# The product of the bias table with the one-hot rows moves from ahead of the first attention scores to among the first idle products

## The chip, the cores and the metric

The kernel runs on one core of a Trainium2 chip. The core has five engines, each with its own queue of instructions: TensorE (PE, matrix products), VectorE (DVE), ScalarE (ACT), GpSimd (POOL) and SyncE (SP, which here only issues transfers). Engines wait for one another by semaphores. Sixteen DMA engines move data between HBM and SBUF. The metric is the device time of one execution in microseconds (us).

## The reference, cut to what matters

Two transformer blocks of width 1024 over 256 tokens. The first has a short convolution and a compressed, selected and windowed attention; the second a differential attention, a gated linear attention and a pooling mixer; each ends in a gated feed-forward part. The changed part computes one small thing of the second block, the bias of a score by the distance of query and key:

```python
bias_by_dist = rel_bias[t5_bucket(jnp.arange(S))]          # 256 distances x 4 heads
...
dist = jnp.arange(q0, kend)[:, None] - jnp.arange(kend)[None, :]
bias = bias_by_dist[jnp.clip(dist, 0, S - 1)].astype(jnp.float32)
s = s + jnp.transpose(bias, (2, 0, 1))[None, :, None]
s = jnp.where(dist[None, None, None] >= 0, s, -1e30)
```

## The kernel before, in words

All order is written out by hand, one instruction list per engine, in `program`. TensorE holds x transposed (AA) and multiplies it by weights that come from HBM in units of up to 1 MB. SyncE issues the units in the order of the list `units` into a ring of four buffers (RAW, `NRAW`). A unit is issued when the unit four places ahead has been split (`split_lo`). ScalarE makes a unit's rounded high part (HI, `hi`, L538) and VectorE the rest (LO, `lo`, L1002), each in two halves, into rings of three; TensorE waits for the half it needs (`unit_ready`).

The first units are, in order: keys of the windowed branch (0), the two for the compressed blocks (1, 2), the gates (3, 192 KB), query weights (4), the first layer of the key compression (5, 6), query weights (7), the value compression (8, 9), query weights (10, 11) and values (12). TensorE goes through them in the function under `@block.tensor`: `queries(0, ...)` uses unit 4, `hidden(0)` units 5 and 6, `queries(1, ...)` unit 7, `hidden(1)` units 8 and 9, `queries(2, ...)` unit 10. After `values(U_VALS, ...)` the attention of the first block begins, in which projections (units 13 and on) fill the time between its small steps.

Until x is there, TensorE has nothing to do and runs idle products (`idle(n)`, L1639): 14, then the two that spread the gain `g_mix` over the partitions (L1646), then 13, then the first turns of the normalized x (L1633).

The bias table takes this way. GpSimd loads the constant one-hot rows (OH, 33 x 384) and the table (REL, 32 x 4; its row 32 is set to -1e30 for distances below zero). TensorE multiplies them (L1781) into 4 x 384 bias values in bank B[0], behind the values and ahead of the first scores. ScalarE writes them back into the first four rows of OH (L649). GpSimd then issues `bias_rows` (L456), a transfer that writes each of the four rows 128 times to HBM:

```python
e.wait_ge(setup, HMASK)
e.wait_ge(rel_sb, 1)
e.dma_start(bias_rows.rearrange("h r n -> h (r n)").rearrange("h (r n) -> h r n", n=ROW),
            OH[0:4, :].unsqueeze(1).to_broadcast([4, 128, ROW])).then_inc(bias_moved, 16)
```

It is read back skewed (L468) when the scores of the first attention are done, at 225.9 us. On GpSimd's queue all instructions run in order: first `ones`, `ident` and ROOT, then loads of small rows (VR), the first root (`root(1, ...)`, the inverse root of x's mean square), more loads, masks, the loads of OH and REL, later small loads, two loads of gains (GB, 512 KB each as written), the memsets of `hmask`, and `bias_rows`.

Of the kernel before, what the change touches and what calls it, by code (L numbers as in the profile page):

```python
# [17 lines left out]
NEG = -1.0e30  # L18
# [3 lines left out]
ROW = 384  # L22
# [37 lines left out]
def program(nc, A, out):  # L60
    with ExitStack() as ctx:
# [3 lines left out]
        def sem(name):  # L65
            return ctx.enter_context(nc.semaphore("s_" + name))
# [86 lines left out]
        rows_in, first_in, second_in = sem("rows_in"), sem("first_in"), sem("second_in")  # L153
        FIRST_IN, SECOND_IN = 80, 64
        bias_moved, out_done = sem("bias_moved"), sem("out_done")

        setup = sem("setup")
        ONE, IDENT, HALF, IDENTB, MASKF, MASKC, KC0, VB0, UP0, GMASK, FAR, HMASK = 1, 3, 4, 6, 8, 10, 11, 12, 13, 16, 17, 22
        gate_sb = sem("gate_sb")
# [19 lines left out]
        ck_pe, ck_sb, cv_pe, cv_sb = sem("ck_pe"), sem("ck_sb"), sem("cv_pe"), sem("cv_sb")  # L179
        rel_pe, rel_sb = sem("rel_pe"), sem("rel_sb")  # L180

        score_pe, masked_sb, most_sb, exp_sb = sem("score_pe"), sem("masked_sb"), sem("most_sb"), sem("exp_sb")
# [199 lines left out]
        def _(e):  # L382
# [10 lines left out]
            def root(n, dst, src, k=2):  # L393

                e.wait_ge(mean_sb, n)
                e.tensor_tensor(dst, src, ROOT[:, 0:k], ALU.pow).then_inc(root_sb, 1)

            e.dma_start(VR[0:12, :], A["conv_w"][0].rearrange("k (c p) -> (k c) p", p=128)).then_inc(rows_in, 16)
            e.dma_start(VR[12:28, :], A["cmp_pos_k"][0].rearrange("(l a) d -> l (a d)", a=2)).then_inc(rows_in, 16)
            e.dma_start(VR[28:44, :], A["cmp_pos_v"][0].rearrange("(l a) d -> l (a d)", a=2)).then_inc(rows_in, 16)  # L400
            e.dma_start(VR[44:46, :], A["pool_scale_2"][0, :].rearrange("(c p) -> c p", p=128)).then_inc(rows_in, 16)
            e.dma_start(VR[46:47, :], A["gla_gate_b_2"]).then_inc(rows_in, 16)
            e.wait_ge(setup, HALF)
            root(1, ST[:, 6:8], ST[:, 4:6])
# [28 lines left out]
            for h in range(2):  # L433
                e.affine_select(out=gmask[h * 64:h * 64 + 64, :], in_=gmask[h * 64:h * 64 + 64, :], compare_op=ALU.is_ge,
                                fill=0.0, base=0, pattern=[[1, 64]], channel_multiplier=-1).then_inc(setup, 1)
            e.dma_start(OH[:, :], A["c_onehot"]).then_inc(first_in, 16)
            e.dma_start(REL[0:32, :], A["rel_bias_2"]).then_inc(first_in, 16)
            e.wait_ge(setup, GMASK)
            e.memset(REL[32:33, :], NEG).then_inc(setup, 1)
            e.dma_start(LV[:, :, :], A["lambda_vecs_2"][0].rearrange("a d -> (a d)").partition_broadcast(128)  # L440
# [7 lines left out]
            gain(1, A["g_ffn"][0, :])  # L448
            e.wait_ge(setup, FAR)
            e.memset(hmask[:, :], 0.0).then_inc(setup, 1)  # L450
            e.wait_ge(setup, FAR + 1)
            for h in range(4):
# [71 lines left out]
        def _(e):  # L524
# [40 lines left out]
            def keys(br, c):  # L565
                e.wait_ge(keys_pe, 2 * br + c + 1)
                e.activation(KT[:, br, c, :], B[c][:, 0:S], ACT.Copy).then_inc(keys_sb, 1)

            def values(br, t):
                e.wait_ge(vals_pe, 2 * br + t + 1)  # L570
                e.activation(VV[:, br, t, :], B[t][:, 0:256], ACT.Copy).then_inc(vals_sb, 1)

            keys(0, 0)
            hi(2, 0)
# [72 lines left out]
            values(0, 1)  # L647
            e.wait_ge(rel_pe, 1)
            e.activation(OH[0:4, :], B[0][0:4, 0:ROW], ACT.Copy).then_inc(rel_sb, 1)  # L649

# [905 lines left out]
        def _(e):  # L1556
# [79 lines left out]
            def idle(n):  # L1636

                for _ in range(n):
                    e.matmul(B[7][:, 0:128], ones[:, :], ones[:, :], start=True, stop=True)  # L1639
# [7 lines left out]
            x.then_inc(gain_pe, 1)  # L1647
            idle(13)
            e.wait_ge(setup, IDENT)
# [127 lines left out]
            for t in range(2):  # L1777
                values(U_VALS, 0, t)
            e.wait_ge(setup, FAR)
            take(0, rel_sb, 1)  # L1780
            e.matmul(B[0][0:4, 0:ROW], REL[:, :], OH[:, :], start=True, stop=True).then_inc(rel_pe, 1)  # L1781

# [478 lines left out]
```

## Time and profile before

| | |
|---|---|
| device time, median of 3 runs | 747.46 us (746.82 to 747.47) |
| span of the profiled execution | 745.2 us (the page gives no other time of it) |
| TensorE busy | 740.4 us, 99% |
| VectorE busy | 518.0 us, 70% |
| ScalarE busy | 416.4 us, 56% |
| GpSimd busy | 66.5 us, 9% |
| chain that ended last | TensorE 97%, VectorE 2%, ScalarE 1% |
| moved by DMA | 131.26 MB, mean 176 GB/s; 266, 297, 311 and 274 GB/s in the first four of 40 slices |

The span runs from the first to the last instruction of the profiled execution. A row of a timeline gives the start in us from the span's start, the length, the engine, the line and what it writes and reads; "xN" are records merged into one row. An fp32 product leaves two records. The idle time ahead of a row stands in brackets, with what ended it. A DMA's "us to landing" runs from its issue until its semaphore is complete.

### The profile page before, as it was taken

To read this page: it belongs to the slowest core of one execution; us is meant where nothing else is said; L and a number is where in the kernel's file an instruction comes from. 1 tells how busy PE (TensorE), PEld (TensorE's weight loads), DVE (VectorE), ACT (ScalarE), POOL (GpSimd) and SP (SyncE) were. 2 spreads that over 40 slices of the span, in tenths; PEclk is the share of its full clock that TensorE was granted. 3 is DMA by queue.
4 is the path that set the end of the run, shared out by engine and by line. 5 is a ranking of instruction groups with operands and counts; after the bars stand their busy time and mean duration, and the time that the engine had idled before them with its cause. 6 is when DMAs were issued, how large, how long until landed. Compare 5 with 4: busy or idle time off the path is not lost.

```text
span 745.2 us, 11582 instructions
## 1 busy us (share of the span) xinstructions
PE 740.4 (99%) x4563; PEld 641.4 (86%) x4563; DVE 518.0 (70%) x834; ACT 416.4 (56%) x788; POOL 66.5 (9%) x103
## 2 busy tenths in 40 slices
PE   9999999999999999999999999999999999999998
PEld 8999999877888888888888888887888888888886
DVE  5784677885756678887367757898667777447762
ACT  5575557556463455565356546597646656345640
POOL 6300000000010000430000004400100000000000
PEclk9999999999999999999999999999999999999999
DMA  8998444343455546766656461735355655656611
GB/s 266 297 311 274 85 109 153 114 128 123 146 170 197 167 152 222 198 213 228 188 172 212 171 226 54 251 124 174 111 168 170 191 204 174 222 170 188 207 57 56
DMA packets 99209, 131.26 MB, mean 176 GB/s; under 512 B 5357, under 2 KB 79163, under 8 KB 99156
## 3 DMA queue, kind: packets, MB, share of 16 engines
q1 hardware_dynamic: 96564, 125.58, 52.6%
q0 software_dynamic: 2304, 4.43, 2.7%
q8 instruction: 36, 0.59, 0.3%
q10 hardware_dynamic: 288, 0.52, 0.2%
q14 instruction: 17, 0.14, 0.1%
HBM read 128.68 MB, written 1.84 MB: 175 GB/s over the span
## 4 chain that ended last, share of the span: by engine, by line
PE 97%; DVE 2%; ACT 1%; issue 0%; POOL 0%; POOLq 0%
PE B L1626 39%; PE B L1592 22%; PE B L1597 11%; PE B L1581 11%; PE B L1805 2%; PE B L1852 2%; PE B L1815 2%; PE B L1639 1%; PE B L1685 1%; PE B L1633 1%; DVE LO L1002 1%; PE B L1808 1%; PE B L1832 1%; PE B L1730 1%; PE B L1791 0%; PE B L1729 0%
## 5 line engine op out<-in xcount | busy, mean ns | idle before, releaser
L1002 DVE TENSOR_TENSOR LO<-RAW,HI 128x1024 fp32r<-128x1024 f32 x236 | 282.5, 1236 | 101.0 <-ACT HI L538 100.5
L1626 PE MATMUL B<-HI,AA 128*128 128x512 f32 (+1 forms) x960 | 286.8, 376 | 0.3 <-DVE AA L1008 0.2
L538 ACT ACTIVATE HI<-RAW 128x1024 fp32r<-128x1024 f32 (+1 forms) x240 | 237.2, 1038 | 63.1 <-PE B L1626 58.2
L1626 PEld LDWEIGHTS B<-HI,AA 128*128 128x128 f32 x960 | 175.7, 188 | 33.8 <-issue 1.6
L1592 PE MATMUL B<-AA,HI 128*128 128x512 f32 x704 | 179.2, 393 | 0.0
L1626 PE MATMUL B<-LO,AA 128*128 128x512 f32 (+1 forms) x480 | 178.6, 372 | 0.0
L1592 PEld LDWEIGHTS B<-AA,HI 128*128 128x128 f32 x704 | 126.8, 189 | 23.0 <-issue 0.7
L1626 PEld LDWEIGHTS B<-LO,AA 128*128 128x128 f32 x480 | 90.6, 189 | 14.6
L1597 PEld LDWEIGHTS B<-AA,LO 128*128 128x128 f32 x704 | 96.6, 190 | 7.1
L1597 PE MATMUL B<-AA,LO 128*128 128x256 f32 x704 | 98.8, 282 | 0.0
L1581 PE MATMUL B<-AA,HI 128*128 128x256 f32 x448 | 83.3, 287 | 0.0
L1581 PEld LDWEIGHTS B<-AA,HI 128*128 128x128 f32 x448 | 69.8, 191 | 1.1 <-issue 0.4
L1581 PE MATMUL B<-AA,LO 128*128 128x256 f32 x224 | 63.4, 283 | 0.0
L1581 PEld LDWEIGHTS B<-AA,LO 128*128 128x128 f32 x224 | 42.9, 191 | 0.0
L663 ACT ACTIVATE PR<-B,SM 128x128 f32<-128x128 f32 (+1 forms) x64 | 26.3, 427 | 27.6 <-DVE SM L1135 27.6
L793 ACT ACTIVATE SGC<-SGC 128x256 f32<-128x256 f32 x44 | 16.8, 418 | 28.3 <-DVE SGC L1329 28.2
L804 ACT ACTIVATE AA<-SGC 128x256 fp32r<-128x256 f32 x44 | 16.7, 418 | 27.9 <-DVE SGC L1339 27.9
L787 ACT ACTIVATE SGC<-B 128x256 f32<-128x256 f32 x44 | 15.7, 372 | 22.5 <-PE B L1592 22.5
L798 ACT ACTIVATE SGC<-B 128x256 f32<-128x256 f32 x44 | 15.5, 371 | 19.7 <-PE B L1592 19.7
L1135 DVE TENSOR_REDUCE SM<-B 128x2 f32<-128x512 f32 (+1 forms) x24 | 15.4, 683 | 15.2 <-PE B L1808 15.2
L674 ACT ACTIVATE PT<-B 128x512 f32<-128x512 f32 x24 | 14.4, 599 | 18.4 <-PE B L1815 8.8
L1324 DVE TENSOR_TENSOR SGC<-B,SGC 128x256 f32<-128x256 f32 x44 | 17.6, 418 | 8.0 <-ACT SGC L787 7.9
(313 smaller groups left out, 634.9 us busy)
## 6 DMA issues: line engine op xcount, KB each, us to landing
RAW<-in_w_in SPq DMA_DIRECT2D x29, 1024.0 KB, 5.8
RAW<-in_w_gate SPq DMA_DIRECT2D x22, 1024.0 KB, 5.3
RAW<-in_w_up SPq DMA_DIRECT2D x22, 1024.0 KB, 5.3
RAW<-in_w_down SPq DMA_DIRECT2D x22, 1024.0 KB, 5.0
RAW<-in_w_in SPq DMA_DIRECT2D x10, 512.0 KB, 6.4
RAW<-in_w_attn_out SPq DMA_DIRECT2D x4, 1024.0 KB, 5.1
RAW<-in_w_o SPq DMA_DIRECT2D x4, 1024.0 KB, 5.0
RAW<-in_w_out SPq DMA_DIRECT2D x4, 1024.0 KB, 5.0
```

The lines of the kernel that those rows point to most:

```text
L538: e.activation(pieces(HI, NSPL, i, k), pieces(RAW, NRAW, i, k), ACT.Copy).then_inc(split_hi, 1)
L663: x = e.activation(PR[:, k, j * w:j * w + w], sc[:, j, :], ACT.Exp, bias=SM[:, 3 * q, j:j + 1], accum_out=SM[:, 3 * q + 1, j:j + 1])
L787: e.activation(SGC[:, f % 4, :], B[c][:, S:2 * S], ACT.Copy).then_inc(fg_low, 1)
L793: e.activation(SGC[:, f % 4, :], SGC[:, f % 4, :], ACT.Silu).then_inc(silu_sb, 1)
L798: e.activation(SGC[:, 4 + f % 4, :], B[5 + c][:, S:2 * S], ACT.Copy).then_inc(fu_low, 1)
L804: e.activation(AH[:, 8 + f % 12, :], SGC[:, f % 4, :], ACT.Copy).then_inc(ff_hi, 1)
L1002: e.tensor_tensor(pieces(LO, NSPL, i, k), pieces(RAW, NRAW, i, k), pieces(HI, NSPL, i, k), ALU.subtract).then_inc(split_lo, 1)
L1324: e.tensor_tensor(SGC[:, f % 4, :], B[c][:, 0:S], SGC[:, f % 4, :], ALU.add).then_inc(fg_sb, 1)
L1581: x = e.matmul(dst, w[:, t, c0:c0 + n], a, start=(t == 0 and k == 0), stop=(t == nk - 1 and k == 2))
L1592: return e.matmul(dst[:, :], hi[:, t, c0:c0 + 128], flatten(AA[:, ch + t, :, :]), start=(t == 0), stop=(t == nk - 1))
L1597: e.matmul(dst[:, 0:S], lo[:, t, c0:c0 + 128], AH[:, ch + t, :], start=False, stop=False)
L1626: x = e.matmul(dst, a, w[:, t, c0:c0 + n], start=(first and t == 0 and k == 0), stop=(last and t == nk - 1 and k == 2))
```

## The change

The loads of OH and REL become the first transfers of GpSimd, ahead of those of VR, with a semaphore of their own (`rel_in`; `FIRST_IN` falls from 80 to 48). The memset of REL's last row follows them, with the semaphore `far_set` in place of the step FAR of `setup`. The product goes to the second row of idle products, behind 3 of them and ahead of 7 (13 before), and into bank B[4] instead of B[0]. ScalarE's evacuation moves ahead of its first keys. `bias_rows` and everything behind it stay where they are in GpSimd's list.

```diff
--- before.py
+++ after.py
@@ -151,11 +151,11 @@
         raw_in = [sem(f"raw_in{i}") for i in range(NRAW)]
         gain_in = [sem("gain0_in"), sem("gain1_in")]
         rows_in, first_in, second_in = sem("rows_in"), sem("first_in"), sem("second_in")
-        FIRST_IN, SECOND_IN = 80, 64
+        FIRST_IN, SECOND_IN = 48, 64
         bias_moved, out_done = sem("bias_moved"), sem("out_done")
 
         setup = sem("setup")
-        ONE, IDENT, HALF, IDENTB, MASKF, MASKC, KC0, VB0, UP0, GMASK, FAR, HMASK = 1, 3, 4, 6, 8, 10, 11, 12, 13, 16, 17, 22
+        ONE, IDENT, HALF, IDENTB, MASKF, MASKC, KC0, VB0, UP0, GMASK, HMASK = 1, 3, 4, 6, 8, 10, 11, 12, 13, 16, 21
         gate_sb = sem("gate_sb")
         gain2, final_x, normal_x, pool_step = sem("gain2"), sem("final_x"), sem("normal_x"), sem("pool_step")
         states0, scan_ones, lr_act = sem("states0"), sem("scan_ones"), sem("lr_act")
@@ -178,6 +178,7 @@
         hturn_pe, pads = sem("hturn_pe"), sem("pads")
         ck_pe, ck_sb, cv_pe, cv_sb = sem("ck_pe"), sem("ck_sb"), sem("cv_pe"), sem("cv_sb")
         rel_pe, rel_sb = sem("rel_pe"), sem("rel_sb")
+        rel_in, far_set = sem("rel_in"), sem("far_set")
 
         score_pe, masked_sb, most_sb, exp_sb = sem("score_pe"), sem("masked_sb"), sem("most_sb"), sem("exp_sb")
         weight_sb, pturn_pe, pturn_sb, o_pe = sem("weight_sb"), sem("pturn_pe"), sem("pturn_sb"), sem("o_pe")
@@ -395,12 +396,16 @@
                 e.wait_ge(mean_sb, n)
                 e.tensor_tensor(dst, src, ROOT[:, 0:k], ALU.pow).then_inc(root_sb, 1)
 
+            e.dma_start(OH[:, :], A["c_onehot"]).then_inc(rel_in, 16)
+            e.dma_start(REL[0:32, :], A["rel_bias_2"]).then_inc(rel_in, 16)
+            e.wait_ge(setup, HALF)
+            e.memset(REL[32:33, :], NEG).then_inc(far_set, 1)
             e.dma_start(VR[0:12, :], A["conv_w"][0].rearrange("k (c p) -> (k c) p", p=128)).then_inc(rows_in, 16)
             e.dma_start(VR[12:28, :], A["cmp_pos_k"][0].rearrange("(l a) d -> l (a d)", a=2)).then_inc(rows_in, 16)
             e.dma_start(VR[28:44, :], A["cmp_pos_v"][0].rearrange("(l a) d -> l (a d)", a=2)).then_inc(rows_in, 16)
             e.dma_start(VR[44:46, :], A["pool_scale_2"][0, :].rearrange("(c p) -> c p", p=128)).then_inc(rows_in, 16)
             e.dma_start(VR[46:47, :], A["gla_gate_b_2"]).then_inc(rows_in, 16)
-            e.wait_ge(setup, HALF)
+            e.wait_ge(far_set, 1)
             root(1, ST[:, 6:8], ST[:, 4:6])
             for i, n in ((47, "q_norm_g_2"), (48, "k_norm_g_2"), (50, "gla_norm_g_2")):
                 for a in range(2):
@@ -433,10 +438,7 @@
             for h in range(2):
                 e.affine_select(out=gmask[h * 64:h * 64 + 64, :], in_=gmask[h * 64:h * 64 + 64, :], compare_op=ALU.is_ge,
                                 fill=0.0, base=0, pattern=[[1, 64]], channel_multiplier=-1).then_inc(setup, 1)
-            e.dma_start(OH[:, :], A["c_onehot"]).then_inc(first_in, 16)
-            e.dma_start(REL[0:32, :], A["rel_bias_2"]).then_inc(first_in, 16)
             e.wait_ge(setup, GMASK)
-            e.memset(REL[32:33, :], NEG).then_inc(setup, 1)
             e.dma_start(LV[:, :, :], A["lambda_vecs_2"][0].rearrange("a d -> (a d)").partition_broadcast(128)
                         .rearrange("p (a d) -> p a d", a=4)).then_inc(second_in, 16)
             e.wait_ge(pads, 1)
@@ -446,9 +448,8 @@
 
             gain(0, A["g_final"])
             gain(1, A["g_ffn"][0, :])
-            e.wait_ge(setup, FAR)
             e.memset(hmask[:, :], 0.0).then_inc(setup, 1)
-            e.wait_ge(setup, FAR + 1)
+            e.wait_ge(setup, GMASK + 1)
             for h in range(4):
                 e.memset(hmask[32 * h:32 * h + 32, 64 * h:64 * h + 64], 1.0).then_inc(setup, 1)
             e.wait_ge(setup, HMASK)
@@ -570,6 +571,8 @@
                 e.wait_ge(vals_pe, 2 * br + t + 1)
                 e.activation(VV[:, br, t, :], B[t][:, 0:256], ACT.Copy).then_inc(vals_sb, 1)
 
+            e.wait_ge(rel_pe, 1)
+            e.activation(OH[0:4, :], B[4][0:4, 0:ROW], ACT.Copy).then_inc(rel_sb, 1)
             keys(0, 0)
             hi(2, 0)
             keys(0, 1)
@@ -645,8 +648,6 @@
                              B[7][0:15, 0:256].rearrange("p (g d) -> p g d", g=4), ACT.Copy, scale=0.5).then_inc(cv_sb, 1)
             values(0, 0)
             values(0, 1)
-            e.wait_ge(rel_pe, 1)
-            e.activation(OH[0:4, :], B[0][0:4, 0:ROW], ACT.Copy).then_inc(rel_sb, 1)
 
             def exponents(s):
                 k, q = s % 2, s % 3
@@ -1645,7 +1646,12 @@
                 take(2 + h, scaled_sb, 4)
                 x = e.matmul(B[2 + h][:, :], ones[64 * h:64 * h + 1, :], GAIN[64 * h:64 * h + 1, :], start=True, stop=True)
             x.then_inc(gain_pe, 1)
-            idle(13)
+            idle(3)
+            e.wait_ge(rel_in, 32)
+            e.wait_ge(far_set, 1)
+            take(4, rel_sb, 1)
+            e.matmul(B[4][0:4, 0:ROW], REL[:, :], OH[:, :], start=True, stop=True).then_inc(rel_pe, 1)
+            idle(7)
             e.wait_ge(setup, IDENT)
 
             def turns(h):
@@ -1776,9 +1782,6 @@
             queries(3, 1)
             for t in range(2):
                 values(U_VALS, 0, t)
-            e.wait_ge(setup, FAR)
-            take(0, rel_sb, 1)
-            e.matmul(B[0][0:4, 0:ROW], REL[:, :], OH[:, :], start=True, stop=True).then_inc(rel_pe, 1)
 
             def scores(s):
```

TensorE's list at the start, before. B<-ones are the idle products, B<-TMP,ones spread the gain, B<-ident,TOK are the turns of x.

```order
L1639 MATMUL B<-ones 128x128 x13
L1646 MATMUL B<-TMP,ones 128x512 [waits s_row_in]
L1646 MATMUL B<-TMP,ones 128x512
L1639 MATMUL B<-ones 128x128 x13
L1633 MATMUL B<-ident,TOK 128x128 [waits s_scaled_sb,s_setup]
```

The same place after (the lines are one further down).

```order
L1640 MATMUL B<-ones 128x128 x13
L1647 MATMUL B<-TMP,ones 128x512 [waits s_row_in]
L1647 MATMUL B<-TMP,ones 128x512
L1640 MATMUL B<-ones 128x128 x3
L1653 MATMUL B<-OH,REL 4x384 [waits s_far_set,s_rel_in]
L1640 MATMUL B<-ones 128x128 x7
L1634 MATMUL B<-ident,TOK 128x128 [waits s_scaled_sb,s_setup]
```

Between the gain and the turns the product has taken the place of three idle products, with a wait for its inputs.

GpSimd's list from the loads of OH and REL to `bias_rows`, before.

```order
L436 DMA OH<-in_c_onehot 33x384
L437 DMA REL<-in_rel_bias 32x4
L439 MEMSET REL 1x4 [waits s_setup]
L440 DMA LV<-in_lambda_vecs 128x256
L444 DMA GW<-in_gla_gate_w 16x128 [waits s_pads]
L444 DMA GW<-in_gla_gate_w 16x128
L445 DMA PW<-in_pool_w 128x2x64
L384 DMA GB<-in_g_final 128x1024
L384 DMA GB<-in_g_ffn 128x1024
L450 MEMSET hmask 128x256 [waits s_setup]
L453 MEMSET hmask 32x64 [waits s_setup]
L453 MEMSET hmask 32x64 x3
```

The same stretch after, up to `bias_rows`.

```order
L442 DMA LV<-in_lambda_vecs 128x256 [waits s_setup]
L446 DMA GW<-in_gla_gate_w 16x128 [waits s_pads]
L446 DMA GW<-in_gla_gate_w 16x128
L447 DMA PW<-in_pool_w 128x2x64
L385 DMA GB<-in_g_final 128x1024
L385 DMA GB<-in_g_ffn 128x1024
L451 MEMSET hmask 128x256
L454 MEMSET hmask 32x64 [waits s_setup]
L454 MEMSET hmask 32x64 x3
L457 DMA bias_rows<-OH 512x1x384 [waits s_rel_sb,s_setup]
```

Three instructions have left the stretch; `bias_rows` waits for ScalarE's evacuation (s_rel_sb) as before.

ScalarE's list around that evacuation, after; before it had no OH<-B here, and had it behind the VV<-B that follow the values.

```order
L539 ACTIVATE HI<-RAW 128x1024 [waits s_raw_in1]
L539 ACTIVATE HI<-RAW 128x1024
L575 ACTIVATE OH<-B 4x384 [waits s_rel_pe]
L568 ACTIVATE KT<-B 128x256 [waits s_keys_pe]
L539 ACTIVATE HI<-RAW 128x1024 [waits s_raw_in2]
```

The wait for the product now stands ahead of the first keys.

## Rows read from the trace of the kernel before

**Rows 1.** The page, busy time of each engine.
```profile
PE 740.4 (99%) x4563; PEld 641.4 (86%) x4563; DVE 518.0 (70%) x834; ACT 416.4 (56%) x788; POOL 66.5 (9%) x103
```

**Rows 2.** The chain of waits, 38 to 76 us: start, length, what.
```profile
43.63 2.88 PE B L1581 x24
53.58 2.88 PE B L1581 x24
72.92 0.73 PE B L1781 x2
```

**Rows 3.** TensorE's timeline, first 15 us: start, length, what.
```profile
1.06 5.68 PE L1639 MATMUL B<-ones 128*128 128x128 f32 x28 [1.06 <-POOL ones L386]
7.73 3.17 PE L1639 MATMUL B<-ones 128*128 128x128 f32 x26
10.93 1.06 PE L1633 MATMUL B<-ident,TOK 128*128 128x128 f32 x8
```

**Rows 4.** Stretches: PE, PEld, DVE, ACT, POOL busy; PEclk, DMA share, GB/s.
```profile
2.00:3.00 1.00, 1.00 (x7) 1.00 (x6) 0.00 (x0) 1.00 (x1) 1.00 (x2) 1.00 0.75 252
40.00:45.00 5.00, 5.00 (x44) 5.00 (x44) 5.00 (x6) 4.26 (x6) 0.00 (x0) 1.00 1.08 318
```

**Rows 5.** GpSimd's timeline; in brackets the idle time ahead and its releaser.
```profile
9.50 0.71 POOL L396 TENSOR_TENSOR ST<-ST,ROOT 128x2 f32<-128x2 f32 x1 [4.82 <-DVE ST L1037]
20.73 0.56 POOL L436 DMA_DIRECT2D OH<-in_c_onehot  x1
21.91 0.56 POOL L440 DMA_DIRECT2D LV<-in_lambda_vecs  x1
25.69 0.74 POOL L453 MEMSET hmask<- 32x64 f32 x4
74.91 1.13 POOL L456 DMA_DIRECT2D bias_rows<-OH  x1 [48.49 <-ACT OH L649]
```

**Rows 6.** ScalarE's timeline around its first keys.
```profile
19.50 0.38 ACT L567 ACTIVATE KT<-B 128x256 f32<-128x256 f32 x1 [1.82 <-PE B L1685]
```

**Rows 7.** The groups by line, 36 to 46 us, of the split.
```profile
L1002 DVE TENSOR_TENSOR LO<-RAW,HI 128x1024 fp32r<-128x1024 f32 x8 | 9.3, 1219 | 0.0
L538 ACT ACTIVATE HI<-RAW 128x1024 fp32r<-128x1024 f32 x7 | 7.2, 1052 | 1.0 <-DMA RAW<-in_cmp_w_v 1.0
```

**Rows 8.** SyncE's queue: issues of weight units.
```profile
30.73 1.75 SPq L372 DMA_DIRECT2D RAW<-in_w_in  x1
81.26 0.37 SPq L374 DMA_DIRECT2D RAW<-in_w_in  x1
106.91 1.72 SPq L374 DMA_DIRECT2D RAW<-in_w_in  x1
```

**Rows 9.** Issues at 20.7, 24.8, 23.3, 74.9, 81.3, 106.9: KB, us to landing.
```profile
OH<-in_c_onehot POOLq DMA_DIRECT2D x1, 49.5 KB, 4.6
GB<-in_g_ffn POOLq DMA_DIRECT2D x1, 512.0 KB, 8.2
RAW<-in_cmp_w_k SPq DMA_DIRECT2D x1, 1024.0 KB, 8.0
bias_rows<-OH POOLq DMA_DIRECT2D x1, 768.0 KB, 35.1
RAW<-in_w_in SPq DMA_DIRECT2D x1, 1024.0 KB, 30.7
RAW<-in_w_in SPq DMA_DIRECT2D x1, 1024.0 KB, 10.5
```

**Rows 10.** The DMA queues in 76.7:110.0, 81:94, 100:106, 32:33: packets, MB, share.
```profile
q0 software_dynamic: 702, 0.79, 24.1%
...
q1 hardware_dynamic: 780, 0.79, 19.3%
...
q1 hardware_dynamic: 30, 0.03, 1.4%
...
q1 hardware_dynamic: 583, 0.30, 105.7%
```

## The prediction, made before the changed kernel ran

> **What bounds the kernel.** I read the page's busy times first: TensorE is busy for 740.4 of the 745.2 us of the span [rows 1], so whatever stops TensorE costs its full length, and whatever is taken off any other engine costs or gives nothing by itself. Then the chain of waits around both places of the moved product: the product stands in the chain with 0.73 us at 72.92, directly behind the values and ahead of the first scores at 73.65 [rows 2]; so on TensorE it is paid in full today. Then the timelines of the first 15 us of TensorE and GpSimd, to see whether the new place is really free. Last, since the result of the product feeds a transfer, the DMA views: how long that transfer takes, on how many DMA engines, and what the weight stream does meanwhile. This last view decides the case.
>
> **The product on TensorE.** It leaves 72.92 to 73.65, where it takes 0.73 us of the chain [rows 2]. At the start it stands among the idle products that fill the time until the normalized x is there. Of 13 idle products 10 are left; the 13 are 26 records in 3.17 us, 0.244 us each [rows 3], so three fewer give 0.73 us, and the product costs the same 0.73. The turn of x follows the last idle product at 10.93 without a gap [rows 3]; it also needs the two engines' scaling of x, so I give it neither gain nor loss. Sum: 0 at the start, -0.73 us at 72.92. The first scores wait for ScalarE's evacuations of values and keys; these are done or are no later than now, so I take the full 0.73.
>
> **Its inputs.** The two loads are now the first of GpSimd's queue. OH's, issued at about 1.9, took 4.6 us to landing at its old place [rows 9]; REL's follows by one issue of 0.56 us [rows 5]. They land at about 6.5 and 7.1. The product comes to its turn at 7.73 + 0.73 = 8.5: a margin of 1.4 us. I take 0. As the upper end REL's landing may take half as long again (6.9 us, 9.4): 0.9 us. The loads also put 50 KB among the first x and weight transfers; at the 252 GB/s between 2 and 3 us [rows 4] that is 0.2 us of DMA, and I take 0.
>
> **GpSimd's queue.** The two issues and the memset take 1.18 us at their old place (21.91 - 20.73). At the new one they go ahead of five row loads and the first root; the root waits for VectorE until 9.50, with 4.82 us idle before it [rows 5]. That cover hides them. After the root the queue is as now up to 20.73, so the rows for TensorE's turn of VR come no later: 0. From 20.73 on everything is 1.18 us earlier.
>
> **ScalarE.** The evacuation of the product (4 x 384 elements) moves before the first keys, where ScalarE is idle for 1.82 us before 19.50 [rows 6]; a copy of 128 x 1024 takes 1.05 us [rows 7], so even that would be hidden. 0.
>
> **The transfer behind it.** This is what the diff doesn't show. GpSimd's next issue, bias_rows (768 KB, each of four SBUF rows written 128 times), waits for that evacuation: 48.49 us of waiting, issue at 74.91 [rows 5]. After the change nothing holds it: the evacuation is done before the keys' at 19.50, and the issue stands right behind the memsets of hmask, which end at 26.43. So it is issued at 26.43 - 1.18 = 25.25 us, in the densest part of the weight stream, not at the start of attention.
>
> What the transfer does while it runs is in the trace of before. It takes 35.1 us to landing, to 110.0 [rows 9]; its data flow in the stretch from 76.7 to 110.0, that is 33.3 us, at 24.1% of sixteen engines: four engines, fully taken [rows 10]. Three weight units of 1 MB were issued meanwhile, the first at 81.26, the third at 106.91 [rows 8]. These two took 30.7 and 10.5 us [rows 9] and landed at 111.96 and 117.41: none before the transfer's end, then three within 5.45 us, one each 2.7 us. The packets say why: between 81 and 94 us the hardware queue moved 780 packets, and the twelve free engines' part of a unit of 1024 is 768. So the quarter of a unit that falls to the four busy engines got a dozen packets in 13 us; between 100 and 106 us it was 30 [rows 10]. In attention this costs nothing that the chain shows, since units are wanted there only once in some 12 us (two issues in 25.65 us, 81.26 to 106.91, after the first) and the ring is full.
>
> From 25 us on the ring isn't full. The DMA share is 1.08 from 40 to 45 us [rows 4], and ScalarE already waits 1.0 us for weights between 36 and 46 [rows 7]. Which unit is hit? The unit issued at 23.34 is ahead of the transfer and landed 8.0 us later, at 31.3 [rows 9]. The next, the eighth (query weights, in two halves, the second issued at 30.73), comes after it [rows 8]. TensorE begins with this unit at 43.63 [rows 2].
>
> **When the transfer ends.** With nothing ahead its data begin 1.8 us after issue (76.7 - 74.91), at 27.05, and end at 60.4. But two loads of GB stand ahead on the same queue, the second landing 8.2 us after 24.75, at 32.95 [rows 9]. I take 31.3, where both the unit ahead and most of GB are through: end at 64.6. The upper end is 32.95 + 33.3 = 66.3. The eighth unit's last quarter follows with the 2.7 us that lie between landings today (2.0 as the lower end, 111.96 - 110.0; its packets have 512 bytes, of which sixteen engines moved 583 in 1 us [rows 10], so 512 of them on four engines take 3.5 us, the upper end): landing at 67.3, between 62.4 and 69.8. ScalarE's half (1.05 us) and VectorE's (1.22) come before TensorE [rows 7]: 69.6. TensorE stops for 69.6 - 43.63 = 26.0 us, between 21.0 and 28.4. The three units behind it are by then issued and land 2.7 us apart, faster than TensorE uses them (two query halves of 2.9 us and the hidden product): no second stall.
>
> **The restart.** TensorE's first 28 records after its idle start took 203 ns each, the later 26 took 122 [rows 3], while the granted clock's row reads 1.00 (2.4 GHz) for 2 to 3 us as for 40 to 45 [rows 4]. Whatever makes the first ones slow would come again after 26 us of idleness: 28 x 0.081 = 2.3 us. I take it, with 0 as the other end. In attention the weights come sooner than now, which gives nothing, since TensorE didn't wait.
>
> **Sum:** -0.73 + 26.0 + 2.3 = +27.6 us on the 745.2 us of the profiled execution. The page gives no time around that span; the median of the three runs, 747.46, lies 2.3 us above it, and I put the difference on the median: 775.0. The ends: -0.73 + 21.0 = +20.3 (767.8), and -0.73 + 0.9 + 28.4 + 2.3 = +30.9 (778.3).
>
> **Rivals.**
> 1. *The transfer is hidden (on the other side).* If the eighth unit lands by 43.63 - 2.27 = 41.4 us, TensorE never waits, and the removed 0.73 us is all: 746.7, not slower. For it: in attention the same transfer cost TensorE nothing, and the weights are issued from another queue than GpSimd's, so that they may well go on beside it when both have packets. Against it: three landings out of three after the transfer's end [rows 9]. It decides when the quarter on the four engines gets its 512 packets within 10 us; in before it got 12 in 13. Chance 0.07.
> 2. *The engines are shared by turns.* If the four engines gave half of their time to the weights, a unit would take 5.8 us instead of 2.9. From 31.3 on: landings at about 38, 44, 50 and 56; with 2.27 us behind them the first three are about in time, the fourth, wanted at 53.58 [rows 2], is 4.7 us late, and the later ones have more lead. Total -0.7 + 4.7: 751.5. For it: the 30 packets between 100 and 106 us, more than twice the pace of before [rows 10]. Against it: at 5 packets in 1 us the 256 of a unit's quarter still take 51 us. Chance 0.07.
> The Trainium skill (DMA: Bandwidth & Descriptors, section on queues, rings and completion order) says that each DMA engine goes round between its queues packet by packet, a packet being some 9 to 17 descriptors typically. By that rule the weights would get through in a few turns, this rival or better; the trace doesn't agree for this transfer: the unit issued at 81.26 took 30.7 us [rows 9].
> 3. *The inputs come late.* If REL's load lands at 9.4 instead of 7.1, TensorE waits 0.9 us behind the third idle product and shifts all; with the transfer hidden that gives 747.6. Chance 0.01.
>
> **Chances and range.** Forecast 0.85, the rivals 0.07, 0.07 and 0.01. What the runs can tell from no change is 0.2%, 1.5 us. The forecast and rival 2 are slower (0.92), rivals 1 and 3 within it (0.08), of which I give 0.01 to a gain above 1.5 us, for which 72.92 would have to hide more than its 0.73. The forecast's own range is 767.8 to 778.3; where the transfer begins and how its packets mix is the uncertain part, so with some room on both sides I go to 763 and 781.
>
> **What would show it.** In the profile after: bias_rows issued near 25 us and landing near 65; the unit issued at 30.3 landing later still; TensorE idle once, from about 43.6 to 69.7, before a line of query weights, released through VectorE's LO; the product at about 8.5 without a wait; 72.92's 0.73 us gone. Wrong would be: that unit landing before 42 us, or bias_rows starting only when the weight stream has a gap.

## The result, and the profile after

The changed kernel takes 770.82 us (median of 4 runs, 770.28 to 771.99) against 747.14 for the kernel before (4 runs beside it, 746.13 to 747.47). The ratio is 1.0322, with a 95% interval of 1.0309 to 1.0334: slower by 3.2%, where 775.0 (763 to 781) was forecast. The profiled execution's span is 768.7 us, 23.5 above the 745.2 of before. Of all runs in this document one stands in no median: the kernel of experiment 8 once took 1075.91 us, at a mean granted clock of 0.65.

The busy times of the profile's page, which answer to [rows 1]:

```profile
PE 742.3 (97%) x4557; PEld 642.6 (84%) x4557; DVE 518.2 (67%) x834; ACT 416.3 (54%) x788; POOL 66.9 (9%) x103
```

TensorE does the same work (742.3 us against 740.4), but its share of the span has fallen to 97%: the loss is time in which it stands still. Where, the list of TensorE's waits says (line, what was waited for: us in total, times, longest):

```profile
PE B L1582 <- DVE LO L1003: 17.8, 1, 17.8
PE B L1735 <- DVE LO L1003: 3.7, 1, 3.7
PE B L1640 <- POOL ones L387: 1.1, 1, 1.1
```

Two of these are new. The chain of waits names what is behind them (start, length, what):

```profile
30.19 33.41 DMA RAW<-in_w_in
...
63.62 1.06 ACT HI L539
...
64.70 1.24 DVE LO L1003
...
66.08 4.65 PE B L1582 x24
...
71.11 2.92 PE B L1582 x24
...
97.13 1.09 PE B L1808 x16
```

Here stands a transfer of 33.41 us, the second half of the eighth unit, where before there were only products. It lands at 63.6. ScalarE's and VectorE's halves of the split follow, and TensorE goes on at 66.08 with what it did at 43.63 before [rows 2]. The 24 products take 4.65 us there, not 2.88; the granted clock between 66 and 71 us is 0.64, where it was 1.00 at the same products before. From 71.11 on (46.90 before) everything is as before, 24.2 us later, until the scores, which start at 97.13 (73.65 before) without the product's 0.73 us. There the shift is 23.5 us, and it stays so to the end.

The timeline of GpSimd, as [rows 5]:

```profile
1.95 0.76 POOL L399 DMA_DIRECT2D OH<-in_c_onehot  x1 [0.21 <-issue]
2.71 0.54 POOL L400 DMA_DIRECT2D REL<-in_rel_bias  x1
...
8.94 0.72 POOL L397 TENSOR_TENSOR ST<-ST,ROOT 128x2 f32<-128x2 f32 x1 [3.10 <-DVE ST L1038]
...
22.87 0.53 POOL L385 DMA_DIRECT2D GB<-in_g_final  x1
...
24.33 0.74 POOL L454 MEMSET hmask<- 32x64 f32 x4
25.38 1.13 POOL L457 DMA_DIRECT2D bias_rows<-OH  x1 [0.30 <-POOL hmask L454]
```

bias_rows is issued at 25.38, not at 74.91. The DMA view of the issues at 22.8, 25.4, 29.8, 30.2 and 34.5 (KB, us to landing), which answers to [rows 9]:

```profile
RAW<-in_cmp_w_k SPq DMA_DIRECT2D x1, 1024.0 KB, 19.8
...
bias_rows<-OH POOLq DMA_DIRECT2D x1, 768.0 KB, 35.4
...
RAW<-in_w_in SPq DMA_DIRECT2D x1, 512.0 KB, 7.7
...
RAW<-in_w_in SPq DMA_DIRECT2D x1, 512.0 KB, 33.4
...
RAW<-in_cmp_w_v SPq DMA_DIRECT2D x1, 1024.0 KB, 32.0
```

bias_rows lands at 60.8, the half issued at 30.19 at 63.6, the value compression's first unit at 66.5. The half issued at 29.78 was through in 7.7 us. The unit issued at 22.80, which took 8.0 us before, took 19.8 and landed at 42.6: that is the first, shorter stop of TensorE (3.7 us, in the product of the hidden layer). And the queues between 40 and 50 us:

```profile
q0 software_dynamic: 51, 0.24, 23.6%
q1 hardware_dynamic: 38, 0.02, 0.7%
```

The weights' queue gets 38 packets in 10 us, while GpSimd's queue (q0) takes 23.6% of sixteen engines, that is four of them almost without a gap. SyncE's queue shows one more trace of it:

```profile
34.53 24.18 SPq L375 DMA_DIRECT2D RAW<-in_cmp_w_v  x1
58.75 2.86 SPq L375 DMA_DIRECT2D RAW<-in_cmp_w_v  x1
```

The issue itself of the unit at 34.53 took 24.18 us, with the next coming only at 58.75.

At the start of the kernel the product runs where the forecast had it (start, length, what):

```profile
7.24 0.86 PE B L1640 x6
8.11 0.73 PE B L1653 x2
8.84 1.76 PE B L1640 x14
10.60 0.45 PE B L1634 x4
```

3 idle products, the product with 0.73 us at 8.11 without a wait, 7 idle products, the turn of x. All of this is 0.33 to 0.54 us earlier than before, since the first 28 records took 5.12 us and not 5.68 [rows 3]. That isn't the change's: in the kernel of the first experiment below the same 28 took 5.98. It goes with the clock: the trace's first record of it, at 1.00, begins at 4.7 us here, at 5.9 before and at 6.5 in that experiment.

The account of the 23.5 us: start -0.54; stops +3.74 and +17.84; slow products +1.41 up to 66.08 and +1.77 behind it (4.65 - 2.88); the removed product -0.73. Sum 23.49. The 1.41 is a remainder (66.08 - 43.63 = 22.45, less the three terms before) and was not measured by itself; in that stretch, 45 to 50 us, TensorE works for 3.23 us at a granted clock of 0.57.

### The profile page after: what moved, and what is told of

The parts are those of the page before. It is cut to its first block, busy times and chain, and to the rows that moved or that the text cites. A ratio compares the mean times of both kernels' runs of the same rounds, so it can differ in the third digit from the quotient of the medians.

```text
span 768.7 us, 11570 instructions
## 1 busy us (share of the span) xinstructions
PE 742.3 (97%) x4557; PEld 642.6 (84%) x4557; DVE 518.2 (67%) x834; ACT 416.3 (54%) x788; POOL 66.9 (9%) x103
## 4 chain that ended last, share of the span: by engine, by line
PE 92%; DMA 4%; DVE 3%; ACT 1%; issue 0%; SPq 0%; POOL 0%; POOLq 0%
PE B L1627 38%; PE B L1593 21%; PE B L1598 11%; PE B L1582 9%; DMA RAW<-in_w_in 4%; PE B L1808 2%; PE B L1855 2%; PE B L1818 1%; PE B L1640 1%; DVE LO L1003 1%; PE B L1691 1%; PE B L1634 1%; PE B L1811 1%; PE B L1835 0%; PE B L1794 0%; PE B L2078 0%
## 5 line engine op out<-in xcount | busy, mean ns | idle before, releaser
L1582 PE MATMUL B<-AA,HI 128*128 128x256 f32 x448 | 84.8, 290 | 17.8 <-DVE LO L1003 17.8
L664 ACT ACTIVATE PR<-B,SM 128x128 f32<-128x128 f32 (+1 forms) x64 | 26.2, 424 | 28.4 <-DVE SM L1136 28.4
L794 ACT ACTIVATE SGC<-SGC 128x256 f32<-128x256 f32 x44 | 16.7, 418 | 28.3 <-DVE SGC L1330 28.2
L805 ACT ACTIVATE AA<-SGC 128x256 fp32r<-128x256 f32 x44 | 16.7, 418 | 27.9 <-DVE SGC L1340 27.9
```

What stands on the lines that cost most here:

```text
L664: x = e.activation(PR[:, k, j * w:j * w + w], sc[:, j, :], ACT.Exp, bias=SM[:, 3 * q, j:j + 1], accum_out=SM[:, 3 * q + 1, j:j + 1])
L794: e.activation(SGC[:, f % 4, :], SGC[:, f % 4, :], ACT.Silu).then_inc(silu_sb, 1)
L805: e.activation(AH[:, 8 + f % 12, :], SGC[:, f % 4, :], ACT.Copy).then_inc(ff_hi, 1)
L1582: x = e.matmul(dst, w[:, t, c0:c0 + n], a, start=(t == 0 and k == 0), stop=(t == nk - 1 and k == 2))
```

## The experiments

The excerpts leave out declarations, the single issue that a split one replaces, and waits whose counts follow from the edit.

**1. The changed kernel with the early issue taken back.** GpSimd holds bias_rows until the values are copied, where it stood before; all else of the change stays.

```diff
             e.wait_ge(setup, HMASK)
             e.wait_ge(rel_sb, 1)
+            e.wait_ge(vals_sb, 2)
             e.dma_start(bias_rows.rearrange("h r n -> h (r n)").rearrange("h (r n) -> h r n", n=ROW),
```

> The changed kernel, with GpSimd's issue of bias_rows held until ScalarE has copied the second half of the values (where it stood before). All else of the change stays. Theory (the early transfer holds four DMA engines and the weight units wait behind it): both stops of TensorE (3.7 and 17.8 us) and the slow products behind them are gone, what is left is the removed product: 747.1 - 0.7 = 746.4 us. Rival (the stop comes from the moved loads or the wait for them): still about 771. Rival (the product's place hides something): 746.4 would not be reached, 747.1 or more.

Measured: 746.52 us (11 runs) against 747.13, ratio 0.999 (0.9981 to 0.9999). TensorE's waits are those of the kernel before; the two stops are gone:

```profile
PE B L1641 <- POOL ones L387: 1.1, 1, 1.1
PE B L1628 <- DVE AA L1010: 0.2, 1, 0.2
```

So the whole loss hangs on the moment of this one transfer. What is left is the removed product, 0.6 us measured for 0.73; the interval just leaves out 1.

**2. The kernel before with a copy of the transfer added.** Product and bias_rows stay in their old places.

```diff
+            e.memset(CST[0:4, 0:ROW], 0.0).then_inc(dummy_set, 1)
             e.memset(hmask[:, :], 0.0).then_inc(setup, 1)
...
+            e.wait_ge(dummy_set, 1)
+            e.dma_start(dummy_rows.rearrange("h r n -> h (r n)").rearrange("h (r n) -> h r n", n=ROW),
+                        CST[0:4, 0:ROW].unsqueeze(1).to_broadcast([4, 128, ROW])).then_inc(dummy_moved, 16)
```

> The kernel before, with one transfer added: a copy of the shape and size of bias_rows (four SBUF rows, each written 128 times to HBM, 768 KB) from a zeroed tile to a scratch tensor, issued on GpSimd behind the memsets of hmask, near 26.5 us. The product and the true bias_rows stay where they are. Theory: the transfer alone makes the whole loss: 771 + 0.7 + about 1 us for the later issue = 772 to 773 us. Rival (loss needs the moved loads, product or evacuation): 747 to 749.

Measured: 774.54 us, ratio 1.0371 (1.0353 to 1.039). The waits of its TensorE:

```profile
PE B L1588 <- DVE LO L1009: 22.9, 1, 22.9
PE B L1588 <- DVE CG L1215: 1.2, 1, 1.2
```

So nothing of the moved product is needed for the loss; the transfer makes it alone. Here the unit issued ahead of the transfer wasn't held (9.9 us to landing), and the loss stands in one stop of 22.9 us. The total is 1.5 us above what was expected. There is a second stop of 1.2 us, in attention, and the chain ahead of it runs through a weight unit again (start, length, what):

```profile
105.92 32.13 DMA RAW<-in_w_in
```

That is the true bias_rows: a unit beside it takes 32 us, as one did before (30.7). Why TensorE now has to wait for it was not tested; that the ring of units was less far ahead is my guess.

**3. The early transfer in two halves, one late.** 64 repeats early, 64 behind the values.

```diff
+            e.dma_start(bias_rows[:, 0:64, :], OH[0:4, :].unsqueeze(1).to_broadcast([4, 64, ROW])).then_inc(bias_moved, 16)
+            e.wait_ge(vals_sb, 2)
+            e.dma_start(bias_rows[:, 64:128, :], OH[0:4, :].unsqueeze(1).to_broadcast([4, 64, ROW])).then_inc(bias_moved, 16)
```

> The changed kernel, with bias_rows in two halves of 64 repeats: one at the early place, one held until the values are copied. Theory (weights wait until the transfer's end, us for us): the early half ends 16.7 us sooner, at about 44 instead of 60.8; the eighth unit lands near 47 instead of 63.6, TensorE's stops fall from 21.6 to about 6 us and with them part of the slow products: 771 - 16 to 18 = 753 to 755 us. Rival (engines shared, weights run on at a lower pace): the loss is halved only, 758 to 760.

Measured: 755.39 us, ratio 1.0109 (1.0095 to 1.0123). One stop of 6.8 us is left:

```profile
PE B L1583 <- DVE LO L1004: 6.8, 1, 6.8
```

Half of the transfer takes away two thirds of the loss. That is what waiting for the end gives. The early half lands after 18.7 us instead of 35.4, which is 16.7 us less, and the eighth unit lands at 47.4 instead of 63.6, which is 16.2 us less. The first part of the transfer falls into the eighth unit's lead and costs nothing; the rest costs one us for each us. 755.39 lies just above the 753 to 755 expected, and below the 758 to 760 of the rival of shared engines, which falls.

**4. The early transfer in four quarters.** Four issues of 32 repeats, same bytes, same rows.

```diff
+            for r in range(0, 128, 32):
+                e.dma_start(bias_rows[:, r:r + 32, :], OH[0:4, :].unsqueeze(1).to_broadcast([4, 32, ROW])).then_inc(bias_moved, 16)
```

> The changed kernel, with bias_rows at its early place issued as four transfers of 32 repeats each (192 KB) instead of one of 128. Same bytes, same rows. Theory, if each of the four gets other DMA engines: every engine is held for 33.3 / 4 = 8.3 us, the eighth unit (5 us of lead in the kernel before) is 3 to 5 us late: 749 to 752 us. If all four go to the same four engines: as the changed kernel, 771. Rival (it is the 0.79 MB as such in a full stretch, 2.4 us at 330 GB/s): 771 in any case isn't explained; it would give 747 to 749 for both forms.

Measured: 769.81 us, ratio 1.0304 (1.029 to 1.0318). As the changed kernel, and yet not for the reason I had put down for that case. The queues between 35 and 45 us:

```profile
q0 software_dynamic: 57, 0.26, 100.4%
q1 hardware_dynamic: 15, 0.01, 0.4%
```

The four did get other engines: all sixteen are taken (100.4%). But together they move 0.26 MB in 10 us, the 26 GB/s that four engines move alone. Four times the engines, each four times slower. My expectation took the rate for that of the engine (33.3 / 4 us); it is that of something the four rows share. In this kernel the unit issued ahead of the transfer was held too (33.0 us to landing), and the stops are 17.0 us in the hidden layer and 3.3 us before the eighth unit's products.

**5 and 6. What makes the transfer slow.** The added copy of experiment 2 with other sources. Its line was the first; in experiment 5 it reads 128 rows, each written 4 times (second), in 6 four rows that are 32 apart (third).

```diff
-                        CST[0:4, 0:ROW].unsqueeze(1).to_broadcast([4, 128, ROW])
+                        CST[:, 0:ROW].unsqueeze(1).to_broadcast([128, 4, ROW])
+                        CST[0:128:32, 0:ROW].unsqueeze(1).to_broadcast([4, 128, ROW])
```

> The kernel before with the added copy at the early place (as e2_dummy), of the same 768 KB in the same rows of 1536 bytes, but read from 128 SBUF rows, each written 4 times, instead of from four rows, each written 128 times. Theory A (the transfer is slow since its source is four neighbouring SBUF rows): it takes about as long as a weight unit, 3 to 9 us to landing, and TensorE stops little or not: 747 to 750 us. Theory B (writes to HBM in rows of 1536 bytes are slow): as e2_dummy, 774.5 us.

> As e2_dummy, but the four source rows are 32 SBUF rows apart (0, 32, 64, 96) instead of neighbours. If neighbouring rows share one way out of SBUF, four ways now run side by side: up to four times as fast, 8 to 10 us to landing, and 748 to 753 us. If the limit is that of a DMA engine that reads one row again and again, or of four engines as such: 33 us as before, 774.5 us.

Measured: 747.08 us for 128 rows, ratio 0.9994 (0.9985 to 1.0003), no difference to be told; 759.07 us for four spaced rows, ratio 1.0159 (1.0145 to 1.0173). The transfer of the same 768 KB in the three kernels, neighbours (2), 128 rows (5), spaced (6):

```profile
dummy_rows<-CST POOLq DMA_DIRECT2D x1, 768.0 KB, 34.5
```

```profile
dummy_rows<-CST POOLq DMA_DIRECT2D x1, 768.0 KB, 9.3
```

```profile
dummy_rows<-CST POOLq DMA_DIRECT2D x1, 768.0 KB, 20.4
...
q0 software_dynamic: 81, 0.37, 23.6%
```

34.5, 9.3 and 20.4 us to landing. The destination, its rows and the bytes are the same in all three. Experiment 5 changes two things, the source rows and the number of engines (sixteen instead of four); experiment 4 has shown that sixteen engines alone gain nothing on four rows, so the time lies in the source. Spaced rows give 0.37 MB in 8 us, 46 GB/s, on four engines as before (23.6%): twice the pace of neighbours, so neighbours share a way out. It is not the four times that I had named, and the reason is not shown. One reading is a limit of the engine that reads one row again and again, about 12 GB/s. The other is that the four spaced rows share two ways out by pairs. The lengths of single packets (4608 bytes, three copies of a row) favour the second: about 178 ns in experiments 5 and 7 (26 GB/s for one engine), 0.37 us with spaced rows, 0.74 with neighbours on four engines, 2.8 with neighbours on sixteen, in steps of about two, four and sixteen. A copy from rows at other distances would settle it; none was run.

**7. A version made of this.** The product is made 128 rows wide (REL spread by GpSimd to 33 x 128), so that the early transfer can read 128 rows.

```diff
+            e.wait_ge(rel_in, 32)
+            e.tensor_copy(RELW[0:32, :].rearrange("p (h q) -> p h q", h=4),
+                          REL[0:32, :].unsqueeze(2).to_broadcast([32, 4, 32])).then_inc(far_set, 1)
...
-            e.matmul(B[4][0:4, 0:ROW], REL[:, :], OH[:, :], start=True, stop=True).then_inc(rel_pe, 1)
+            e.matmul(B[4][:, 0:ROW], RELW[:, :], OH[:, :], start=True, stop=True).then_inc(rel_pe, 1)
...
+            e.activation(CST[:, 0:ROW], B[4][:, 0:ROW], ACT.Copy).then_inc(rel_sb, 1)
...
+            e.dma_start(bias_rows.rearrange("h (q r) n -> (h q) r n", r=4),
+                        CST[:, 0:ROW].unsqueeze(1).to_broadcast([128, 4, ROW])).then_inc(bias_moved, 16)
```

> The changed kernel with the product made 128 rows wide: GpSimd spreads the table to 33 x 128 (each head's column 32 times), the product of the same 384 columns fills 128 rows of B[4], ScalarE copies them to 128 rows of CST, and bias_rows, at its early place, writes each of the 128 rows 4 times. Theory A: the transfer lands within 10 us, no stop of TensorE beyond 0 to 2 us, the removed product stays: 746 to 749 us. Theory B: about 771 us.

Measured: 746.23 us (11 runs) against 746.9, ratio 0.9993 (0.9984 to 1.0003). The transfer is issued at 26.17, in the full stretch, and lands in 9.9 us; TensorE has no stop there:

```profile
bias_rows<-CST POOLq DMA_DIRECT2D x1, 768.0 KB, 9.9
```

```profile
PE B L1644 <- POOL ones L388: 1.1, 1, 1.1
...
PE B L1657 <- POOL RELW L411: 0.2, 1, 0.2
```

The wait for RELW (0.2 us) is the price of GpSimd's spreading, since the table landed only at 8.2. This version and that of experiment 1 have the lowest medians (746.23 and 746.52). They did not run beside each other, and only the interval of experiment 1 leaves out 1, by a hair.

**8 to 12. Are the products behind the stop slow since TensorE stood still?** The changed kernel with 66, 56 and 100 idle products ahead of the eighth unit, and the changed kernel itself beside them, twice.

```diff
             hidden(0)
+            idle(66)
             queries(1, 0)
```

> The changed kernel with 66 idle products ahead of the first half of the eighth unit, where TensorE stops for 17.8 us. If the products behind the stop are slow because TensorE had stood still (granted clock 0.64 between 66 and 71 us), they keep their full pace now: 24 products in 2.9 us instead of 4.65, about 1.8 us less than the changed kernel beside it. If the slow products come from elsewhere (weights landing while they run): no difference, or more by what the idle products overhang (66 x 0.24 = 15.8 us at full clock, up to 22 where it begins low: then up to 3 us more).

> The changed kernel itself, as the measure for e8_kept_busy on the same chip: 770 to 772 us.

> As e8_kept_busy with 56 idle products instead of 66, so that they end before the eighth unit is there (56 x 0.244 = 13.7 us, some 2 us more while the clock is low, against 17.8 us of standing still). If standing still makes the products behind it slow: 24 products in 2.9 to 3.3 us instead of 4.65, the whole 768.5 to 769.5 us. If it doesn't: 770 to 771 us.

> The changed kernel itself, as the measure for e10_kept_busy_56 on the same chip: 770 to 772 us.

> As e10_kept_busy_56 with 100 idle products. In the profile of e10 the 56 (112 records in 11.9 us, 0.212 us each) ended at 55.7 and TensorE stood still for another 11.0 us, so nothing was kept busy up to the eighth unit. 100 products take 21.2 us, from 43.8 to 65.0, and leave some 1.5 us. If standing still makes the products behind it slow, the 24 products behind them take 2.9 to 3.3 us instead of 4.5 to 5.0, and the whole is 1.2 to 2 us below the changed kernel's 770.2 to 771.5: 768.5 to 770. If it doesn't: 770 to 772.

Measured: 772.0 us with 66, against 770.2 beside it; 770.96 with 56, against 771.5; 774.05 with 100 (769.01 to 776.0). None saved what I had expected of it, and the first two show nothing: in the profile with 56 the idle products end at 55.7 and TensorE stands still for 11.0 us behind them, and of 66 there is no profile that can be set beside the others. The timeline with 56:

```profile
43.78 11.89 PE L1640 MATMUL B<-ones 128*128 128x128 f32 x105
66.69 0.77 PE L1582 MATMUL B<-AA,HI 128*128 128x256 f32 x2 [11.03 <-DVE LO L1003]
```

The one with 100 answers the question of the pace, though not by its total: there the idle products ran on without a gap into the products of the eighth unit. The chain of the kernel with 100, then of the changed kernel run a second time:

```profile
50.79 22.64 PE B L1640 x200
73.43 1.68 PE B L1582 x14
```

```profile
65.78 4.54 PE B L1582 x24
...
70.71 2.92 PE B L1582 x24
```

14 products in 1.68 us are 0.12 us each, where the standing engine starts with 24 in 4.54, 0.19 each. The granted clock goes with it (stretches; the clock is the third number from the end):

```profile
45.00:50.00 5.00, 2.98 (x14) 2.98 (x15) 3.51 (x3) 2.33 (x5) 0.00 (x0) 0.50 0.26 27
...
70.00:75.00 5.00, 5.00 (x46) 5.00 (x45) 4.33 (x4) 2.80 (x4) 0.00 (x0) 1.00 1.08 278
```

```profile
50.00:55.00 5.00, 0.00 (x0) 0.00 (x0) 0.00 (x0) 0.00 (x0) 0.00 (x0) 0.50 0.26 28
...
66.00:71.00 5.00, 5.00 (x32) 5.00 (x33) 3.93 (x5) 4.04 (x5) 0.00 (x0) 0.70 1.07 286
```

After standing still the clock is at its lower level (0.50, 1.2 GHz), and the first products run at it; kept busy it is at 1.00 (2.4 GHz). But the idle products begin late when a stop comes ahead of them, as it did here (4.8 us, and slow behind it), and then they end at 73.4, where the first half of the unit was split by about 67.8. So the total says nothing: the four runs lie between 769.01 and 776.0, and the profile is of the slowest. The lowest lies within the 768.5 to 770 expected for a kept pace, but no profile shows what it did.

The two repeats of the changed kernel (770.2 and 771.5) show one stop of 23.0 and 22.7 us in place of 3.7 and 17.8:

```profile
PE B L1582 <- DVE LO L1003: 23.0, 1, 23.0
```

In both the unit issued just ahead of the transfer landed after 10.7 and 11.8 us, not 19.8. Whether it is caught changes from one execution to the next; the total hardly does, since either way TensorE waits until the eighth unit's landing.

## Why the prediction was right, point by point

The sign, the mechanism and the place were right: the transfer behind the product, four engines fully taken, the eighth unit, the stop ahead of the query weights. Experiments 1 and 2 show it from both sides. 775.0 was forecast, 770.8 measured; the forecast shift of 27.6 us is 3.9 us above the measured 23.7. In the profile the stops came out 4.4 us below the forecast and the earlier start gave another 0.5, while the restart cost 0.9 more, so the errors cancel in a small part.

- *The product, -0.73 us:* right. 72.92's row is gone, the new place costs nothing; experiment 1 measures 0.6 for all of the change but the transfer.
- *The inputs, 0:* right. OH and REL took 4.5 and 4.7 us, landed at 6.5 and 7.4, and the product ran at 8.11 without a wait.
- *GpSimd's and ScalarE's queues, 0:* right. The root still waited 3.10 us; bias_rows was issued at 25.38 (25.25 forecast).
- *The stop, 26.0 us (21.0 to 28.4):* mechanism right, size too large; 21.6 measured, near the lower end. The term that was mis-sized is the end of the transfer, 64.6 against 60.8, and its two parts can be read from the single DMA packets in the trace, since those of bias_rows are the only ones of 4608 bytes in that stretch. Its first packet starts at 30.3, beside the last of GB's (31.4), where I took 31.3; so the loads of GB did stand ahead of it, and "nothing ahead" (27.05) was not the case. From the first packet to landing it took 30.5 us, not the 33.3 of before, and that is the larger part, 2.8 of 3.8 us. Some twenty of its first packets took about 0.18 us each instead of 0.74, which on four engines saves 20 x 0.56 / 4 = 2.8 us. Before, where nothing preceded it on the queue, such a quick start is missing; what makes it is not shown. All the rest of the chain held: the eighth unit 2.8 us behind the transfer's end (2.7), TensorE's start with both splits 2.5 us behind that (2.27).
- *The unit ahead would be spared:* wrong in the profiled execution, where it landed at 42.6 and not at 31.3; right in both repeats of the changed kernel (experiments 8 to 12). It changes where TensorE stops, and hardly how long in all (21.6 us against 23.0 and 22.7, with slow products in between).
- *The units behind are by then issued:* wrong, without a price. The next unit's issue was itself held for 24.18 us. They landed about 3 us apart all the same (63.6, 66.5 and 69.6), and no further stop came behind the eighth unit.
- *The restart, 2.3 us:* it was 3.2 (1.41 + 1.77), as there were two stops. The forecast took the size from the kernel's start, and left open what makes the products slow; the runs show it to go with the granted clock. The 1.00 that it read for 2 to 3 us [rows 4] is no measurement: that trace has no record of the clock before 5.9 us, and the view prints 1.00 where there is none.
- *Rival 1, hidden:* would need the unit by 41.4; it came at 63.6. *Rival 2, shared by turns,* 751.5: fell, and experiment 3 speaks against it by itself. The Trainium skill's rule of turns by packets (DMA: Bandwidth & Descriptors, section on queues, rings and completion order) could be read so; the trace has 38 weight packets in 10 us against 51 of the other queue, so turns may well be taken, but the other queue's packets last 0.74 us each there, and with such turns 256 packets of a unit's quarter would not get through before the transfer's end. *Rival 3, late inputs:* did not occur.

## What to carry to other kernels

An instruction that is moved forward takes with it all that waited for it. Before moving a small product into a free place, look up what its result releases, and on which engines and in which stretch that will then run; here one added wait on the transfer (experiment 1) is the difference between +3.2% and a small gain. A transfer is judged by how long it holds its engines, not by its bytes: 768 KB from four neighbouring SBUF rows held four engines for 30 to 33 us and cost 24 us, the same 768 KB from 128 rows cost nothing that could be measured.

## What the runs showed of the hardware

- Four neighbouring SBUF rows as a source give some 24 to 26 GB/s, whether four DMA engines read them (0.24 MB in 10 us) or sixteen (0.26 MB in 10 us). Four rows 32 apart give 46 GB/s on four engines. Packets of 4608 bytes took about 0.74 us in the first case, 2.8 in the second, 0.37 in the third, and 0.18 from 128 rows on sixteen engines.
- Splitting such a transfer into four issues spread it over all sixteen engines and gained nothing that can be told (769.8 against 770.8 us), since every engine was then held.
- Weight units issued 4.8 and 9.2 us after such a transfer landed only behind its end: 33.4 and 32.0 us to landing instead of 5 to 8. The unit issued 2.6 us ahead of it took 19.8 us in one profile of the changed kernel, 10.7 and 11.8 in the two others. SyncE's queue itself stood in an issue for 24.18 us.
- TensorE's granted clock fell to 0.50 while it stood still for 23 us in two profiles of the changed kernel; the first 24 products behind the stop took 4.5 to 5.0 us instead of 2.9 in all three. In the first of them it had fallen right behind the shorter stop of 3.7 us: 0.57 between 45 and 50 us, with TensorE at work for 3.23 us of them.
